# Rotary position of a query in the attention of a decoder step: two halves added on VectorE, or kept apart in 128 rows of the score product

## What is computed

```python
q = (c_q @ w_q_up).reshape(B, L, N_HEADS, D_NOPE + D_ROPE)
q_nope = q[..., :D_NOPE]
q_pe = _apply_rope(q[..., D_NOPE:], cos[:, None, :], sin[:, None, :])
k_pe = _apply_rope(k_pe, cos, sin)          # one rotary key for all heads
...
s = (jnp.einsum('bqhn,bkhn->bhqk', q_nope[:, q0:q1], k_nope[:, :q1])
     + jnp.einsum('bqhd,bkd->bhqk', q_pe[:, q0:q1], k_pe[:, :q1])).astype(jnp.float32) * scale
mask = pos[q0:q1, None] >= pos[None, :q1]
p = jax.nn.softmax(jnp.where(mask, s, -jnp.inf), axis=-1).astype(v.dtype)
outs.append(jnp.einsum('bhqk,bkhv->bqhv', p, v[:, :q1]))

def _apply_rope(x, cos, sin):
    x1, x2 = xf[..., :half], xf[..., half:]
    return jnp.concatenate([x1 * cos - x2 * sin, x2 * cos + x1 * sin], axis=-1)
```

## Time and profile before

| | us |
|---|---|
| median of three runs | 1588.17 |
| lowest and highest run | 1585.96, 1592.44 |
| span of the profiled execution | 1590.6 |
| TensorE busy | 1497.3 (94%) |
| VectorE busy | 772.5 (49%) |
| ScalarE busy | 603.5 (38%) |
| POOL busy | 356.2 (22%) |

### The profile page before, as it was taken

One profiled execution on the slowest core, in us unless ns is written; L12 is line 12 of the kernel. 1 busy time (PEld: TensorE's weight loads), 2 busy tenths in 40 slices (PEclk: granted clock), 3 DMA queues, 4 the chain that ended last, 5 costly groups with the idle time before them and its releaser, 6 DMA issues.

```text
span 1590.6 us, 32114 instructions
## 1 busy us (share of the span) xinstructions
PE 1497.3 (94%) x11463; PEld 1418.5 (89%) x11463; DVE 772.5 (49%) x1234; ACT 603.5 (38%) x1085; POOL 356.2 (22%) x422
## 2 busy tenths in 40 slices
PE   5978998889999999999999998789999999999997
PEld 5966676688887999999999998789999999999997
DVE  3876656555553543442334454964444423344332
ACT  6444545475553333311233333342333311233233
POOL 0286776344310002200022132000012200122000
PEclk9999999999999999999999999889999999999998
DMA  7123323333433123223232565512222232222321
GB/s 178 24 59 87 100 79 101 111 97 91 116 91 116 55 84 88 79 85 87 71 87 79 179 153 159 191 35 80 79 80 79 79 93 79 80 79 85 87 67 60
DMA packets 245283, 147.62 MB, mean 93 GB/s; under 512 B 42072, under 2 KB 239615, under 8 KB 244191
## 3 DMA queue, kind: packets, MB, share of 16 engines
q1 hardware_dynamic: 237826, 138.35, 30.1%
q0 software_dynamic: 6704, 7.20, 1.8%
q10 hardware_dynamic: 684, 1.18, 0.2%
HBM read 128.42 MB, written 18.26 MB: 92 GB/s over the span
## 4 chain that ended last, share of the span: by engine, by line
PE 85%; DVE 8%; ACT 3%; issue 3%; DMA 1%; SPq 0%; ACTq 0%; DVEq 0%
PE bank L856 62%; PE bank L776 7%; PE bank L1114 3%; PE bank L1079 3%; PE bank L919 2%; PE bank L979 2%; PE bank L936 1%; PE bank L967 1%; DVE arena L2050 1%; DVE tmpa L2339 1%; ACT arena L1375 1%; DVE arena L2366 1%; DVE sq L2339 1%; DVE tmpa L2048 1%; DVE tmpa L2047 1%
## 5 line engine op out<-in xcount | busy, mean ns | idle before, releaser
L856 PE MATMUL bank<-arena_parts,wR 128*128 128x288 f32 x4224 | 566.0, 296 | 4.2 <-ACT arena_parts L1452 3.7
L856 PEld LDWEIGHTS bank<-arena_parts,wR 128*128 128x128 f32 x4224 | 562.9, 188 | 5.2 <-issue 4.9
L856 PE MATMUL bank<-side_parts,wR 128*128 128x288 f32 x3360 | 447.3, 295 | 1.1 <-DVE tmpa L2411 1.1
L856 PEld LDWEIGHTS bank<-side_parts,wR 128*128 128x128 f32 x3360 | 445.5, 188 | 1.5 <-issue 1.3
L1859 DVE TENSOR_TENSOR wR<-wraw,wR 128x1024 fp32r<-128x1024 f32 x159 | 232.8, 1464 | 241.5 <-ACT wR L1438 240.1
L741 POOL TENSOR_TENSOR arena_parts<-sq,arena_parts 128x576 f32 x64 | 91.6, 1431 | 729.8 <-ACT arena_parts L1669 729.8
L1438 ACT ACTIVATE wR<-wraw 128x1024 fp32r<-128x1024 f32 x159 | 167.0, 1050 | 202.0 <-PE bank L856 187.5
L1375 ACT ACTIVATE arena<-bank 128x256 f32<-128x256 f32 (+9 forms) x223 | 95.3, 443 | 135.0 <-PE bank L776 87.9
L1666 ACT ACTIVATE tmpa<-bank 128x576 f32<-128x576 f32 x64 | 41.7, 651 | 195.5 <-PE bank L856 195.5
L2262 DVE TENSOR_TENSOR sq<-tmpa 128x576 f32<-128x576 f32 x64 | 48.5, 759 | 127.2 <-ACT tmpa L1666 127.2
L2190 DVE TENSOR_TENSOR kpR<-bank,rstd 128x576 f32<-128x576 f32 x32 | 24.2, 758 | 127.9 <-PE bank L856 127.9
(11 more groups left out here) (300 smaller groups left out, 1604.6 us busy)
## 6 DMA issues: line engine op xcount, KB each, us to landing
wraw<-in_mlp_w SPq DMA_DIRECT2D x128, 512.0 KB, 4.0
side<-in_cache_ckv SPq DMA_DIRECT2D x128, 128.0 KB, 2.1
wraw<-in_ssm_w_glu SPq DMA_DIRECT2D x16, 512.0 KB, 4.0
s_state_to_out<-side SPq DMA_DIRECT2D x16, 256.0 KB, 2.5
s_in_to_state<-yblk SPq DMA_DIRECT2D x8, 512.0 KB, 2.6
s_in_to_out<-side SPq DMA_DIRECT2D x64, 64.0 KB
wraw<-in_mla_w_o SPq DMA_DIRECT2D x8, 512.0 KB, 5.2
side<-s_in_to_state SPq DMA_DIRECT2D x2, 2048.0 KB, 13.2
```

Source lines behind the costliest of these rows:

```text
L856: return pe.matmul(bank[:, a, 0:HALF], wR[:, s, wp, k, :], tokens(k, xp)[:, a * HALF:(a + 1) * HALF], start=(first and j == 0), stop=(last ...
```

## The change

The two products of the rotation are no longer added before the scores. One multiplication over all 128 rows writes the whole of `qT[:, h, :]`: nope, rotary times cosine, swapped times sine. The rotary key stands in rows 64 to 95 and again in 96 to 127 of `kT`, so that the score product over 128 rows, in place of 96, adds the two parts. For that, `ropeq[0:64]` receives scale times norm once before the pairs. The sample tokens still need the sum: a small product puts the swapped part of their 64 columns at partitions 64 to 95 (`swapped_part`, in the unused first 128 columns of `ropek`), and the two copies to `QPE` become additions. The semaphore `qr_sb` goes; `qs_sb` takes VectorE's own wait for the small product.

```diff
--- before.py
+++ after.py
@@ -174,6 +174,7 @@
         cq_lo = [[wrawR[:, at + HALF * a:at + HALF * a + HALF] for a in range(2)] for at in (3 * 1024, 0, 2 * 1024, 2 * 1024 + N)]
         cq_lo[3][1] = cq_tail
         wkv = view(2 * 2 * P).rearrange("p (r c h n) -> p r c h n", r=2, c=2, h=2)
+        swapped_part = ropek[64:96, 0:2 * NS].rearrange("p (h n) -> p h n", h=2)
         ukT = view(4 * P).rearrange("p (a n) -> p a n", a=4)
         probs_area = view(2 * SEQ)
         probs = [probs_area[:, 0:SEQ], probs_area[:, SEQ:2 * SEQ], side[:, 8192:8192 + SEQ]]
@@ -291,7 +292,7 @@
         kpe_raw = sem("kpe_raw")
         nat_done, nat_sb = sem("nat_done"), sem("nat_sb")
         hw_in, wq_hi, wq_lo, cq_hi = sem("hw_in"), sem("wq_hi"), sem("wq_lo"), sem("cq_hi")
-        q_done, qn_sb, qr_sb = sem("q_done"), sem("qn_sb"), sem("qr_sb")
+        q_done, qn_sb, qs_sb = sem("q_done"), sem("qn_sb"), sem("qs_sb")
         k_done, k_sb, v_done, v_sb = sem("k_done"), sem("k_sb"), sem("v_done"), sem("v_sb")
         uk_done, uk_sb, ql_done, ql_sb = sem("uk_done"), sem("uk_sb"), sem("ql_done"), sem("ql_sb")
         s_done, nm_ready, p_exp, p_sb = sem("s_done"), sem("nm_ready"), sem("p_exp"), sem("p_sb")
@@ -916,8 +917,7 @@
                 pe.wait_ge(p_sb, p * 8 + (before(u, 3) + CREDIT))
                 n = (blk + 1) * P
                 bank = score_banks[u % 3]
-                pe.matmul(bank[:, 0:n], qT[0:HD, h, blk * P:(blk + 1) * P], kT[0:HD, h, 0:n],
-                          start=True, stop=False)
+                pe.matmul(bank[:, 0:n], qT[:, h, blk * P:(blk + 1) * P], kT[:, h, 0:n], start=True, stop=False)
                 pe.matmul(bank[:, blk * P:n], ident16[:, :], cmask16[:, :], start=False, stop=True).then_inc(s_done, 1)
 
             def unit_turn(p, u):
@@ -985,7 +985,6 @@
                 if isinstance(p, int) and p == 0:
                     keys_product(p)
                 pe.wait_ge(qn_sb, p * 2 + 1)
-                pe.wait_ge(qr_sb, p * 2 + 1)
                 pe.wait_ge(k_sb, p * 2 + 1)
                 pe.wait_ge(kpe_raw, 1)
                 unit_scores(p, 0)
@@ -1002,7 +1001,6 @@
                 ins.then_inc(uk_done, 1)
 
                 pe.wait_ge(qn_sb, p * 2 + 2)
-                pe.wait_ge(qr_sb, p * 2 + 2)
                 pe.wait_ge(k_sb, p * 2 + 2)
                 unit_scores(p, 1)
                 pe.wait_ge(uk_sb, p + 1)
@@ -2009,8 +2007,9 @@
             dve.wait_ge(tile_free, T_B)
             own(tt(kpR[64:96, :], tmpa[64:96, 0, :], tmpa[64:96, 1, :], ALU.add))
             settle()
-            for h in range(2):
-                ins = dve.tensor_copy(kT[64:96, h, :], kpR[64:96, 0:SEQ])
+            for at in (64, 96):
+                ins = dve.tensor_copy(kT[at:at + ROPE, :, :],
+                                      kpR[64:96, 0:SEQ].unsqueeze(1).to_broadcast([ROPE, 2, SEQ]))
             ins.then_inc(kpe_raw, 1)
             dve.wait_ge(rstd_ready, 2)
             own(tt(ropeq[64:128, :], ropeq[64:128, :], rstd[64:128, :], ALU.mult))
@@ -2038,21 +2037,20 @@
                 dve.tensor_scalar(probs[c][:, 0:n], score_banks[c][:, 0:n], stat[:, 32 + c:33 + c], None, ALU.mult)\
                     .then_inc(p_sb, 1)
 
+            own(dve.tensor_scalar(ropeq[0:NOPE, :], rstd[0:NOPE, :], SCALE, None, ALU.mult))
+            settle()
             with dve.Fori(0, PAIRS) as p:
-                step.enter(p, 4 + 8)
+                step.enter(p, 8)
                 for h in range(2):
                     dve.wait_ge(q_done, p * 2 + (h + 1))
-                    dve.scalar_tensor_tensor(out=halves(qT[0:NOPE, h, :]), in0=pair[h][0:NOPE, :, 0:HALF], scalar=SCALE,
-                                             in1=halves(rstd[0:NOPE, :]), op0=ALU.mult, op1=ALU.mult).then_inc(qn_sb, 1)
-                    own(tt(halves(tmpa[64:96, 0, :]), pair[h][64:96, :, 0:HALF], halves(ropeq[64:96, :]), ALU.mult))
-                    own(tt(halves(tmpa[64:96, 1, :]), pair[h][96:128, :, 0:HALF], halves(ropeq[96:128, :]), ALU.mult))
-                    settle()
-                    tt(qT[64:96, h, :], tmpa[64:96, 0, :], tmpa[64:96, 1, :], ALU.add).then_inc(qr_sb, 1)
-                    dve.wait_ge(qr_sb, p * 2 + (h + 1))
+                    tt(halves(qT[:, h, :]), pair[h][:, :, 0:HALF], halves(ropeq[:, :]), ALU.mult).then_inc(qn_sb, 1)
+                    tt(swapped_part[:, h, :], pair[h][96:128, 1, HALF - NS:HALF], ropeq[96:128, SEQ:N], ALU.mult).then_inc(qs_sb, 1)
+                    dve.wait_ge(qs_sb, p * 2 + (h + 1))
                 unit_max(p, 0)
+                dve.wait_ge(qn_sb, p * 2 + 2)
                 for h in range(2):
-                    dve.tensor_copy(QPE[0:ROPE, :].rearrange("p (t h) -> p t h", h=HEADS)[:, :, ds(p * 2 + h, 1)],
-                                    qT[64:96, h, SEQ:N].unsqueeze(2)).then_inc(ql_sb, 1)
+                    tt(QPE[0:ROPE, :].rearrange("p (t h) -> p t h", h=HEADS)[:, :, ds(p * 2 + h, 1)],
+                       qT[64:96, h, SEQ:N].unsqueeze(2), swapped_part[:, h, :].unsqueeze(2), ALU.add).then_inc(ql_sb, 1)
                 unit_max(p, 1)
 
                 def latent_queries():
```

## The result

The changed kernel takes 1576.4 us (median of 5 runs, 1573.01 to 1579.84) against 1588.17 (5 runs): a ratio of 0.9919, 95% interval 0.9895 to 0.9942, or 11.8 us less. The forecast of 1581.6 us had little more than half of that, and its range for 8 in 10 (1576.5 to 1587.0) ended 0.1 us above the result. The profiled execution is that of 1573.01 us, its span 1571.3; the profile before is of an execution of 1592.44 us.

What follows compares the result with a forecast made beforehand. TensorE was taken as nearest the bound in the attention stage, its waits deciding: 4.9 + 1.2 + 0.5 = 6.6 us off 1588.17 gives 1581.6 us. Own range 1579.4 to 1584.6; 8 in 10, 1576.5 to 1587.0.

Steps and rivals of the forecast that it cites:

- A: TensorE's idle time before the first score product, pairs 1 to 7: 4.9 of 5.57 us gained, ends 4.2 and 5.6.
- B: Wait before the second score product, limited by ScalarE's key-weight copy before L1013: 1.2 us gained, ends 0 and 1.4.
- C: One-time preparation ahead of pair 0: its first score product starts earlier, 0.5 us gained, ends -0.6 and 1.8.
- the strict reading of the port rule: Preparation: both key copies and the added scaling wait for ports shared with GpSimd; 0.6 us lost, sum 5.5 us.
- I put that at nothing: Score product streaming 128 rows for 96: no added time, judged from L967's 593 ns against L919's 658.
- the clock decides, for the better: Attention pairs: a denser pair start might keep the clock up in pairs 4 and 7; 4.1 us more, 1577.5; chance 0.20.
- the sparse stretch behind L1013 stays: Argument against a clock gain: the stretch where TensorE waited on softmax lies behind L1013 and remains; no size given.
- The wait moved: Score products start early, but L1013 or the next pair's weights come no sooner: 1587.7 us; chance 0.15.
- the rival that it would fall in all: Attention pairs: six undisturbed pairs slow down like pair 7, 15 us lost and 6.6 gained: 1596.6 us; chance 0.05.

Runs made afterwards that it cites:

- after again: The changed kernel unchanged, run once more beside other runs on the same chip: 1574.48 us, 0.9909 of the kernel before.
- before again: The kernel before, unchanged, run once more for its clock: 1588.69 us, ratio 0.9991.
- late rotation: The changed kernel with four unused products and a settle put ahead of the first head's rotation: 1585.32 us, 0.9980 of the kernel before.

## Why the prediction was wrong

**The first score product (A, 4.9; ends 4.2 and 5.6) was right in kind and too small.** The first L1013 before, its like after, and pair 1's stretch before:

```profile
99.04 1.10 PE L1013 MATMUL bank<-arena 64*128 64x64 f32 x8 [0.40 <-ACT arena L1375]
```

```profile
97.34 1.23 PE L1011 MATMUL bank<-arena 64*128 64x64 f32 x8
```

```profile
127.18:143.42 16.24, 13.84 (x99) 8.49 (x99) 10.05 (x29) 10.54 (x34) 8.66 (x12) 1.00 0.41 123
```

From the first L1013 to the last the kernel before took 295.26 - 99.04 = 196.22 us, the changed one 284.03 - 97.34 = 186.69, or 9.53 less. Off go pair 4's low clock, 1.66 (17.26 - 15.60), and a wait of 0.64 at full clock in pair 1 (16.24 - 15.60): 7.2 us for A and B in place of 6.1. From the first score product to L1013 it is 3.58 in place of 3.69, so B is 0.8 (7 x 0.11) and A 6.5. The idle time of the earlier trace rows was fully gained, and more: without a wait the score product starts 0.16 us before the row's modelled end of the query products (120.06 + 0.70 against 120.60). That overlap is lost with each wait and does not show as idle: 7 x 0.16 = 1.1, and 5.57 + 1.1 = 6.7. Nothing of the 0.1 us a pair that A left over was there.

**The second score product (B, 1.2; ends 0 and 1.4)** lies inside its ends. As it said, ScalarE's copy stands behind it: L1011 waits 0.59 us for it now.

**The preparation (C, 0.5; ends -0.6 and 1.8)** lies inside too. The first score product comes 13.34 us after the first query product in place of 14.65, but in the profiled execution part of that went to the clock behind it: L1011 comes 19.29 us after it in place of 19.68, 0.4 gained, and 18.48 in after again, 1.2. The two copies took 3.00 us together and L2015 1.71, while the added scaling took 0.45: the strict reading of the port rule, that all three wait, did not come.

**The step that failed is the one on the score product's 128 rows in place of 96: "I put that at nothing".** It is nothing in the product's own length (256 columns took 405 ns in the mean over 96 rows and 406 over 128), but not for the clock, for which the sum had no term. What the rows are worth there is 4.0 us with the waits of before (the kernel before with 128 rows, the fills taken off) and 11.6 us without them (the changed kernel against its 96-row form). The waits alone, 7.2 + 0.4 = 7.6 us, would have given 1580.6, within the forecast's own range.

The rival "the clock decides, for the better" (0.20) came about, at about the 4.1 us it named. Its reason was not the right one: a denser start of the pair does not keep the clock up, as the 96-row run without waits shows. And the argument against it, that the sparse stretch behind L1013 stays, was true and beside the point: the stretch stayed as sparse in time, and its products now have more rows. That its size fits is in part luck: the 4.1 us are what pairs 4 and 7 had lost in one profile, and before again lost 6.8 in pairs 0, 1 and 6.

7.2 + 0.4 in the waits and 4.2 in the clock of pairs 4 and 7 make 11.8 us, as between the medians. This too is in part luck, for the medians beside after again lie 14.0 us apart (1588.46 and 1574.48), and the two profiled executions differ by more (1592.44 and 1573.01): 1.3 us at the head of the program, where the granted clock was 0.96 and then 1.00, and 5.5 behind the attention stage lie where nothing was changed. These were not followed up.

**The other rivals.** The wait moved only in part: L1011 took up 0.59 us. The clock fell in none of pairs 1 to 7, against the rival that it would fall in all. With 96 rows something of that rival would have come: there five of eight pairs ran slow without the waits, and the gain was 2.4 us in all.

## What to carry to other kernels

Where TensorE has to live through a sparse stretch, read the row counts of its products there as well as their times: filling unused rows with zeros cost nothing in the length of the products here and kept the clock at 2.4 GHz behind that stretch; the fills themselves cost 2.4 us once, where they stood in the way. A gain from removed waits is safe only if the clock holds, so compare the granted clock stage by stage before booking it. Where a wait is removed, book the overlap of successive products with the row's idle time.

## What was not expected of the hardware

- With the same instructions, columns and busy time (4.18 and 4.13 us of some 5.4), 96-row score products were followed by a granted clock of 0.50 and 128-row ones by 1.00. Not every pair fell with 96 rows (11 of 28), but none did with 128 (0 of 42). The medians for 128, 96 and 64 rows are 1574.5, 1586.0 and 1619.5 us.
- Rows that hold zeros on one side of the product count too: in the profile of the kernel before with such rows no pair ran at a lower clock from L1013 on.
- Waits of 0.5 to 1.3 us ahead of the score products, in that kernel and in the late rotation, did not bring the clock down; waits of 5.0 and 8.0 us in pair 0 were followed by 0.67 and 0.58.
